# One decoder layer on one core: four in-place softmax buffers with one more task of look-ahead, and router logits taken from un-normed rows

## The reference

```python
h = rmsnorm(xp, ln1_g)
u, va, q, k, v = project(h, w_in, pos)            # five groups of 512 columns, rope on q and k
a_out = sgu_prompt(u, va, sgu_norm_g, sgu_w, sgu_b)
# three dilated windows of attention, merged by their softmax denominators
b_out = merge_by_denominator(outs, lses)
xp = xp + concat(a_out, b_out) @ w_out
h2 = rmsnorm(xp, ln2_g)                           # y * rsqrt(mean(y^2) + eps) * gain
# router: 4 group logits and 32 expert logits of each row
pg = softmax(h2 @ w_rg + b_rg); le = h2 @ w_re + b_re
# top-1 group, top-2 of its 8 experts; the gated MLPs of the chosen experts; sum, final norm
```

## Time and profile before

| | us |
|---|---|
| median of 3 runs (480.13 to 482.16) | 481.65 |
| the profiled execution's own time | 479.57 |
| its span, first to last instruction | 477.6 |

### The profile page before, as it was taken

The page is one execution under the profiler, slowest core; times in us unless marked ns, Lnnn a source line. Parts: engine busy times, 40 slices in busy tenths (PEclk is TensorE's granted clock), DMA queues, the critical chain, the costliest instruction groups (busy, mean ns, idle before and its releaser), DMA issues. The chain is left out here.

```text
span 477.6 us, 5935 instructions
## 1 busy us (share of the span) xinstructions
PE 383.8 (80%) x2256; PEld 197.4 (41%) x2256; DVE 224.8 (47%) x424; ACT 145.6 (30%) x307; POOL 70.4 (15%) x59
## 2 busy tenths in 40 slices
PE   0999996997699898988989999515999999978300
PEld 0554542442243333444544555314555555545100
DVE  1877356999567436356352322470222222211197
ACT  4724022224234336443433112301222222211142
POOL 0000302733140100000000000110223232301100
PEclk9999998899799899999999999855999999989855
DMA  8682422965600746700026791894799999994284
GB/s 298 213 304 64 159 88 71 349 197 188 254 1 2 258 140 183 257 1 1 2 58 281 250 380 44 310 409 178 257 383 413 410 412 407 407 404 160 72 341 176
DMA packets 39201, 104.87 MB, mean 220 GB/s; under 512 B 5656, under 2 KB 6552, under 8 KB 39168
## 3 DMA queue, kind: packets, MB, share of 16 engines
q1 hardware_dynamic: 32736, 89.99, 51.2%
q0 software_dynamic: 5856, 12.81, 7.2%
q10 hardware_dynamic: 576, 1.64, 1.0%
HBM read 97.86 MB, written 14.81 MB: 236 GB/s over the span
## 5 line engine op out<-in xcount | busy, mean ns | idle before, releaser
L1397 PE MATMUL bank<-weights_split,tokens_split 128*128 128x512 f16 (+1 forms) x744 | 176.1, 390 | 5.5 <-DVE weights_split L930 4.2
L1397 PEld LDWEIGHTS bank<-weights_split,tokens_split 128*128 128x128 f16 (+1 forms) x744 | 70.1, 98 | 98.1 <-issue 19.1
L1640 PE MATMUL bank<-big,tokens_split 128*64 128x256 f32 x384 | 47.6, 404 | 6.8 <-DMA big<-in_w_up 5.3
L593 POOL TENSOR_TENSOR big<-big,middle 128x1536 f32<-128x1536 f32 x8 | 28.0, 3495 | 104.2 <-DMA middle<-sample_q 54.6
L1640 PEld LDWEIGHTS bank<-big,tokens_split 128*64 128x64 f32 x384 | 30.9, 145 | 20.2 <-issue 7.2
L1303 DVE TENSOR_TENSOR middle<-bank,middle 128x128 f32<-128x128 f32 x16 | 4.7, 292 | 66.1 <-ACT middle L861 66.1
L778 ACT ACTIVATE middle<-bank 128x128 f32<-128x128 f32 (+3 forms) x32 | 13.9, 435 | 49.7 <-PE bank L1445 49.7
L1372 PE MATMUL bank<-ident,big 128*128 128x128 f32 (+1 forms) x92 | 14.6, 294 | 16.5 <-DVE big L940 12.0
L1009 DVE CUSTOM_DVE_ANT_0 middle<-bank,big 128x128 f32<-128x128 f32 (+3 forms) x32 | 15.5, 487 | 22.0 <-PE bank L1437 21.8
L627 POOL DMA_INDIRECT tokens_split<-h_rows,middle x16 | 16.2, 1012 | 64.3 <-PE bank L1629 48.8
L1445 PE MATMUL bank<-ident,middle 128*128 128x128 f32 x80 | 15.5, 291 | 12.3 <-DVE middle L1018 12.3
(11 more groups left out here) (174 smaller groups left out, 486.6 us busy)
## 6 DMA issues: line engine op xcount, KB each, us to landing
big<-in_w_gate SPq DMA_DIRECT2D x12, 1024.0 KB, 11.4
big<-in_w_up SPq DMA_DIRECT2D x12, 1024.0 KB, 14.1
big<-in_w_down SPq DMA_DIRECT2D x12, 1024.0 KB, 12.5
middle<-in_w_in SPq DMA_DIRECT2D x16, 512.0 KB, 6.0
big<-in_cache_win_k SPq DMA_DIRECT2D x24, 256.0 KB, 3.9
middle<-in_cache_win_v SPq DMA_DIRECT2D x24, 256.0 KB, 4.6
big<-in_w_out SPq DMA_DIRECT2D x8, 512.0 KB, 6.5
big<-expert_rows SPq DMA_DIRECT2D x8, 512.0 KB, 6.7
```

The costliest lines, as they stand in the source:

```text
L593: nc.gpsimd.tensor_tensor(prod[:, :, :], kring[:, b % 2], qb[:, b % 2, :].unsqueeze(1).to_broadcast([P, NPAT, W]), ALU.mult).then_inc(prod ...
L1397: ins = T.matmul(out, (hT if rows is None else rows)[:, high_low, k if rows is None else k - 4, tokens], wg[:, place, part, k, columns], s ...
L1640: ins = T.matmul((ptb, ovb)[b][e * CAP:(e + 1) * CAP, 0:2 * FE], xT[:, b, k, e * CAP:(e + 1) * CAP], places[slot][:, 0:2, e, k * FE:(k + 1 ...
```

## The change

Attention: `s_sb` and `p_sb` (two buffers each) become `sp_sb`, four buffers in the same place, in which mask, exponential and scaling are done in place. ACT's list has `exps(n+2)` behind `copy_pt(n)`; DVE's has `add_mask(n+3)` and `scale_p(n+2)`; PE's scores stand in odd tasks, and the scores of tasks 2 and 3 move from task 0 to a place between the va projections of tiles 0 and 1. `add_mask(2)` and `scale_p(1)` stand ahead of the loop on DVE. One transpose of the mixed rows moves from task 27 to 28.

Router: the router weights are multiplied by the gain once (on DVE, in task 5), the transposes and products take the rows x as they are, and the factor of the row is put on the 36 logits of a row (`logits`). The norm written to memory is made in three pieces: DVE multiplies each half of a row tile by the gain (`times`), ACT squares each half into a PSUM bank and takes the root, and ACT multiplies the row by the factor (`scale_h2`). The logits of a tile go to SBUF tile by tile, from two banks in turn. The sample rows' transposes get a place of their own.

```diff
-TURN_AFTER = {27: ("sgu", 0), 29: ("sgu", 1), 30: ("sgu", 2), 31: ("sgu", 3)}
+TURN_AFTER = {28: ("sgu", 0), 29: ("sgu", 1), 30: ("sgu", 2), 31: ("sgu", 3)}
...
-        s_sb = cut(att, 0, 2, 512)
-        p_sb = cut(att, 1024, 2, 512)
+        sp_sb = cut(att, 0, 4, 512)
...
-            sp.dma_start(wr[:, :, :], w_router).then_inc(consts_in, 16)
+            by_chunk = w_router.rearrange("p k n -> (p k) n").rearrange("(c p) n -> p c n", p=P)
+            sp.dma_start(wr[:, :, :], by_chunk).then_inc(consts_in, 16)
+            sp.dma_start(gcol[:, :], ln2_g.rearrange("(c p) -> p c", p=P), allow_slow_non_contiguous=True).then_inc(gcol_in, 16)
...
+            exps(1)
...
-                if n + 1 < len(TASKS):
-                    exps(n + 1)
+                if n + 2 < len(TASKS):
+                    exps(n + 2)
...
+            def square2(t, half):
+                n, cols_ = rows_of(t), slice(half * 512, (half + 1) * 512)
+                left(act, ("out", 2 * t + half))
+                total = stat[0:n, 64 + t:65 + t] if half == 0 else stat[0:n, 16 + t:17 + t]
+                nc.scalar.activation(sbk[half][0:n, :], x[0:n, t, cols_], ACT.Square, scale=D ** -0.5,
+                                     accum_out=total).then_inc(sq2, 1)
+            def scale_h2(t):
+                n = rows_of(t)
+                act.wait_ge(rms_inverse, t + 1)
+                act.wait_ge(times_gain, 2 * t + 2)
+                rows = h2n[0:n, t % 2, :]
+                nc.scalar.activation(rows, rows, ACT.Copy, scale=stat[0:n, 16 + t:17 + t]).then_inc(h2_ready, 1)
+            for t in range(3):
+                square2(t, 0); square2(t, 1); root2(t)
+                turn_x2(t, 0); turn_x2(t, 1); scale_h2(t)
...
+            square2(NT - 1, 0); turn_x2(NT - 1, 0); square2(NT - 1, 1)
+            turn_x2(NT - 1, 1); root2(NT - 1); scale_h2(NT - 1)
...
-                if n >= 2:
-                    dve.wait_ge(exp_done, n - 1)
+                if n >= 4:
+                    dve.wait_ge(p_turned, n - 3)
...
+            add_mask(2)
             scale_p(0)
+            scale_p(1)
...
-                if n + 2 < len(TASKS):
-                    add_mask(n + 2)
+                if n + 3 < len(TASKS):
+                    add_mask(n + 3)
...
-                if n + 1 < len(TASKS):
-                    scale_p(n + 1)
+                if n + 2 < len(TASKS):
+                    scale_p(n + 2)
...
+            def times(t, half):
+                n = rows_of(t)
+                if half == 0 and t >= 2:
+                    dve.wait_ge(h2w[t - 2], 16)
+                left(dve, ("out", 2 * t + half))
...
+            def logits(t):
+                n = rows_of(t)
+                dve.wait_ge(r_done, t + 1)
+                dve.wait_ge(rms_inverse, t + 1)
+                V.scalar_tensor_tensor(out=L[0:n, t, :], in0=(ptb, ovb)[t % 2][0:n, 0:36],
+                                       scalar=stat[0:n, 16 + t:17 + t], in1=rbias[0:n, :],
+                                       op0=ALU.mult, op1=ALU.add).then_inc(logits_done, 1)
...
+            step(V.memset(L[:, NT - 1, :], 0.0))
             add_out(0, 0)
             add_out(1, 0)
...
+            for t in range(2, NT):
+                add_out(t, 0)
+                times(t, 0)
+                first_half(t - 1)
+                inverse(t - 1)
+                logits(t - 2)
...
+                add_out(t, 1)
+                times(t, 1)
+            inverse(NT - 1)
+            logits(NT - 2)
+            logits(NT - 1)
...
             scores(0)
             for t in range(NT):
                 project(("va", t))
+                if t == 0:
+                    scores(1)
...
-                if n % 2 == 0 and n + 2 < len(TASKS):
-                    scores(n // 2 + 1)
+                if n % 2 == 1 and n + 3 < len(TASKS):
+                    scores((n + 3) // 2)
...
+            x_turns(0, 0); x_turns(0, 1); project_out(2, 0)
+            router(0, 0); router(0, 1); x_turns(1, 0); x_turns(1, 1); project_out(2, 1)
+            router(1, 0); router(1, 1); project_out(3, 0)
+            x_turns(2, 0); x_turns(2, 1); project_out(3, 1)
+            router(2, 0); router(2, 1); x_turns(3, 0); project_out(4, 0)
+            x_turns(3, 1); project_out(4, 1); router(3, 0); router(3, 1)
+            x_turns(4, 0); router(4, 0); x_turns(4, 1); router(4, 1)
```

More of the change, by code:

```diff
@@ L820, in _, with root2, turn_x2 @@
             act.dma_start(gain[:, :], ln2_g.partition_broadcast(P)).then_inc(gain_in, 16)
[L822 to L833, removed]
+            def square2(t, half):
[4 more added lines that the diff above has]
+                                     accum_out=total).then_inc(sq2, 1)
+            def root2(t):
+                n, v = rows_of(t), stat[0:rows_of(t), 16 + t:17 + t]
+                act.wait_ge(sq2, 2 * t + 2)
+                act.wait_ge(half_ms, t + 1)
+                nc.scalar.activation(v, v, ACT.Sqrt, bias=stat[0:n, 64 + t:65 + t]).then_inc(rooted, 1)
+            def turn_x2(t, c):
+                if t == NT - 1:
+                    turn(("h2", 2 * t + c), x_sampleT[:, 4 * c:4 * c + 4, :])
+                    return
                 if t >= 1:
@@ L837, in turn_h2 @@
                     act.wait_ge(acc_ready, UNIT[("mix", 3)] + 1)
[L838 to L843, removed]
+                turn(("h2", 2 * t + c), h2T[:, 4 * c:4 * c + 4, :])
+            def scale_h2(t):
[5 more added lines that the diff above has]
+            for t in range(3):
+                square2(t, 0)
+                square2(t, 1)
+                root2(t)
+                turn_x2(t, 0)
+                turn_x2(t, 1)
+                scale_h2(t)
+            square2(3, 0)
+            turn_x2(3, 0)
+            square2(3, 1)
+            root2(3)
+            turn_x2(3, 1)
+            scale_h2(3)
+            square2(NT - 1, 0)
+            turn_x2(NT - 1, 0)
+            square2(NT - 1, 1)
+            turn_x2(NT - 1, 1)
+            root2(NT - 1)
+            scale_h2(NT - 1)
             act.wait_ge(gexp_in, 1)
@@ L1163, in _, with first_half @@
+            def first_half(t):
+                v = stat[0:rows_of(t), 64 + t:65 + t]
+                dve.wait_ge(sq2, 2 * t + 1)
+                V.tensor_scalar(v, v, EPS, None, ALU.add).then_inc(half_ms, 1)
+            dve.wait_ge(pv_done, len(TWOS))
+            step(V.memset(L[:, NT - 1, :], 0.0))
             add_out(0, 0)
             add_out(1, 0)
[L1165 to L1168, removed]
-                add_out(t, 1)
[L1170 to L1180, removed]
+            dve.wait_ge(gain_in, 32)
@@ L1187, in over_r @@
                 return v.unsqueeze(1).to_broadcast([P, t, v.shape[1]])
[L1188 to L1193, removed]
             L4 = L[:, :, 0:NG]
@@ L1584, in _ @@
             project_out(1, 1)
-            h2_turns(0)
-            for t in range(2, NT):
-                project_out(t, 0)
-                router(t - 2)
-                project_out(t, 1)
-                h2_turns(t - 1)
-            router(NT - 2)
-            h2_turns(NT - 1)
-            router(NT - 1)
+            pe.wait_ge(wr_scaled, 1)
+            x_turns(0, 0)
+            x_turns(0, 1)
+            project_out(2, 0)
+            router(0, 0)
+            router(0, 1)
+            x_turns(1, 0)
+            x_turns(1, 1)
+            project_out(2, 1)
+            router(1, 0)
+            router(1, 1)
+            project_out(3, 0)
+            x_turns(2, 0)
+            x_turns(2, 1)
+            project_out(3, 1)
+            router(2, 0)
+            router(2, 1)
+            x_turns(3, 0)
+            project_out(4, 0)
+            x_turns(3, 1)
+            project_out(4, 1)
+            router(3, 0)
+            router(3, 1)
+            x_turns(4, 0)
+            router(4, 0)
+            x_turns(4, 1)
+            router(4, 1)
             pe.wait_ge(picks, 1)
```

64 lines of the change are left out of this document (48 added, 16 removed).

## The result

The kernel after takes 468.02 us (median of 4 runs, 467.43 to 468.91), the kernel before beside it 480.89 (480.13 to 482.16): the ratio is 0.9731, 95% interval 0.97 to 0.9763. The profiled execution of after took 468.41, its span is 466.5.

The account below looks back on a forecast made before the run. PE was taken to set the pace, its waits being what could be won: attention 6.0 + output tail 2.5 − first gather 0.6 = 7.9 us, giving 473.7 us. Range 469.0 to 478.0; the forecast's own 471.5 to 476.

Parts of the forecast that it names:

- 5.9 + 0.6: Attention: look-ahead removes eight transpose waits, +5.9 us; moved scores fill the wait for the u weights' split, +0.6.
- The 1.0 us of waits left standing: Attention: of the eight waits' 6.9 us, 1.0 stays for ACT's copy and the seventh task; bounds 0 and 3.0.
- The new wait: Near 90 us: moved scores of tasks 2 and 3 make PE wait 3.1 us for the first pair's masks.
- the case that the sum took with 1.2: New wait brings 3.4 us of half clock; attention starts 1.2 us later, the middle of 0.4, 1.2 and 2.9.
- the 2.9 worked out for that case: New wait brings 6.8 us of half clock; attention starts 2.9 us later.
- The backlog of weights: Rival, chance 0.15: first gather's rows land only when the weights' queue is through; tail gives nothing, 476.1 us.
- the first gather: Before the experts: issued earlier into a full DMA, takes the median 7.4 us instead of 6.8; −0.6 (−1.5 to 0).
- Router(1): Output projection: router products of tile 1 may wait behind the memory write of tile 0; 0.2 us taken.
- the attention's sum: Attention: 5.9 + 0.6 + 0.7 − 1.2 = +6.0 us (1.7 to 7.8).
- kinder clock: Rival, chance 0.16: half-clock stretches near 159 and 121 go or halve, new wait brings none; 4.2 us more, 469.5.
- The tail: Last projection's end to first logits reduction: 5.2 us instead of 8.2.
- The 0.5 us by which the last projection should end later: Output projection: added transposes, memset and router wait, less a saved norm wait, end the last projection 0.5 us later.

Follow-up runs that it names:

- the two added waits: After with two PE waits added where it had none, GpSimd multiplying an idle SBUF stretch at tasks 18 and 26; 475.29 us, ratio 0.9871.
- the repeat: After unchanged, timed again on the same chip beside two later kernels; 468.56 us, ratio 0.9733 to before.
- the kernel of 459.35 us: After with scores 2 and 3 behind the second va tile, second v tile before the first transposes, other v tiles respaced, u split one task earlier; 459.35 us.

## Why the prediction was off

**What held.** The waits went as worked out: 5.9 + 0.6 = 6.5 us forecast, 6.5 measured (8.99 less 2.47 of idle time). The 1.0 us of waits left standing came too, though half of it by luck: 0.48 for ACT's copy, as reasoned, and 0.51 for a mask, which the prediction did not name. The scores of tasks 2 and 3 left the path. The new wait came at its place, for the mask; it was 4.57 us in this execution and 3.6 to 4.5 in five others, not 3.1. PE came there sooner than in the earlier trace rows: in after's profile its half clock before that lasted 3.4 us, to 84.7. The start, counted from the transposes near 80, shifted by 1.1 to 1.2 us in the three profiles in which 3.4 us of half clock followed the new wait, the case that the sum took with 1.2. Where 6.8 us followed, it shifted by 1.6 (after's profile) and 2.6 (the two added waits), less than the 2.9 worked out for that case. The product behind the later tile took 0.69 us, not 2.93. The backlog of weights did not hold the first gather: 7.0 us from issue to PE, near the 7.4 taken. Router(1) did not wait.

**The step that failed** is in the attention's sum: it took the 2.08 us wait as shortened to 1.4 and paid only for its length. The two stretches of half clock, behind that wait and behind the entry, were left as they were; the "kinder clock" held them, with a chance of 0.16 and 4.2 us. Two of its three parts came. The stretch near 159 vanished with its wait, which gave the 1.7 us put there. The one at the entry halved when that wait went from 5.40 to 2.64 us; this gave 0.8 and not 1.7, as 1.9 us of before's stretch lay inside the wait. Together that is half of 4.96 us, 2.5 us of the 2.9 by which the attention with its start beat its sum (8.9 against 6.0). It was not chance of one execution: waits of 5.40 to 5.62 us at the entry stood with 6.8 us of half clock in three of three profiles, waits of 2.62 to 2.65 with 3.4 in five of five, and a wait of 2.07 or 2.08 for the u weights with 3.4 in four of four. The third part, no half clock behind the new wait, did not come. The rows already held the evidence: in the earlier trace rows the clock fell behind 2.08 us and not behind 1.64. With such rows a wait that shrinks across that gap should be priced with its stretch. Some 0.8 us of PE's shorter busy time I can't attribute; ends of products are modelled.

**Two terms were mis-sized**, both in the output stage. The tail was put at 5.2 us and took 4.33: the half routers of the sample rows take 0.43 each, not 0.6, and the steps overlap where I added hand-overs of 0.4. The 0.5 us by which the last projection should end later was 0.0, as router(1) did not wait and the other changes cancelled. So +3.8 in place of +2.5. The range had each of these upsides, the clock's 4.2 and the tail's 0.5, but not both at once; 469.0 as its lower end left no place for that. Each stage alone also passed the upper bound of its own sum: 8.9 against 7.8 in the attention (its terms add up to 7.9), and 3.8 against 3.0 in the output stage.

The sum to the first experts' rows in the two profiles: 8.9 in the attention with its start, 3.8 in the output stage, -0.2 for the gather, 12.5 us, where 6.0, 2.5 and -0.6 were forecast; the medians are 12.9 apart.

## What to carry to other kernels

A wait of TensorE is to be priced with what the clock does behind it: look up in the windows whether a stretch of 0.50 follows waits of its length, and count half of that stretch with it, in a gain as in a loss. The longest waits are the first place for work that is ready. A wait ahead of a step that another engine sets costs only what arrives at that step, and removed by itself it may come back there as a longer one; here that one was then filled with work, in the kernel of 459.35 us, among other edits. When work moves between steps that several in-order engines share, look into which step each of its ends falls: one tile that ended a task earlier made a circle of waits over three engines.

## What was not expected of the hardware

Between the first va tile and the end of the output projection the stretches of half clock in these runs went mostly by the length of PE's wait before them: up to 1.85 us none was followed by half clock; of those from 2.03 to 2.65 us most were, by 3.4 us of it, but one of 2.29 us, for split weights at 115 to 117, was not, in four runs; those of 3.4 to 4.0 us were followed by 3.4 or 6.8 us, and not by their order (3.83 us by 3.4, 3.45 us by 6.8); those of 4.5 us and more by 6.8. Behind the last projection, where PE's waits stand close together, the clock fell in before at 305.74, behind waits of 0.80 and 1.70 us: there the list does not hold.

The wait near 80, 3.46 to 3.48 us in all thirteen profiles, shows that length alone does not fix the stretch: it stood with 3.4 us of half clock in six of them and 6.8 in seven. After's two profiles have one of each, the first here and the repeat:

```profile
81.26:84.67 3.41, 3.28 (x11) 1.41 (x12) 2.29 (x2) 1.02 (x2) 0.00 (x0) 0.50 0.90 260
```

```profile
79.81:86.64 6.83, 5.88 (x18) 2.72 (x19) 3.98 (x6) 1.54 (x2) 0.74 (x1) 0.50 0.70 196
```

So the same wait of the same kernel can bring 3.4 us more of half clock, half of it lost for PE, in one execution than in another.
